# First attention of a two-block kernel: its weights turned by VectorE in 32x32 blocks with transfers through DRAM, its value products two units later, and the first block's tokens scaled once

## The reference, cut to what matters

```python
h = rms_norm(x, ln1_g)
z_a, z_b, z_c, z_g = split(h @ w_in)
# branch a: gelu, layer norm, chunked spatial gating, @ w_a_out
# branch b: p * sigmoid(g), causal depthwise convolution of 31 taps, layer norm, silu, @ w_b_out
# branch c, stick breaking attention, 8 heads of 64, for query block i:
z = einsum(q_blk, k[:ctx]) * scale
log_a = log_sigmoid(z) + (cs[..., -1:] - cs)      # cs: running sum of masked log_sigmoid(-z)
a = where(mask, exp(log_a), 0)
out = einsum(a, v[:ctx])                          # then @ w_c_out
merged = sum of sigmoid(z_g + b_gate) * y of the branches
x = x + merged @ w_out                            # then a feed-forward part
```

## Time and profile before

| | |
|---|---|
| median of 3 runs | 1275.33 us (1275.14 to 1275.87) |
| the profiled execution | 1275.76 us, its span 1274.0 us |
| TensorE busy | 1263.9 us, 99% of the span |
| VectorE, ScalarE, GpSimd busy | 869.3, 586.3 and 88.1 us |
| mean granted clock of TensorE | 0.999 |
| 16 DMA engines | 153.36 MB, 40.7% of their time by SP's queue |

### The profile page before, as it was taken

One profiled execution on the slowest core, in us unless ns is written; L12 is line 12 of the kernel. 1 busy time (PEld: TensorE's weight loads), 2 busy tenths in 40 slices (PEclk: granted clock), 3 DMA queues, 4 the chain that ended last, 5 costly groups with the idle time before them and its releaser, 6 DMA issues.

```text
span 1274.0 us, 15378 instructions
## 1 busy us (share of the span) xinstructions
PE 1263.9 (99%) x5760; PEld 1016.6 (80%) x5760; DVE 869.3 (68%) x1164; ACT 586.3 (46%) x866; POOL 88.1 (7%) x68
## 2 busy tenths in 40 slices
PE   8999999999999999999999999999999999999998
PEld 7888777888888888888888888888877777777886
DVE  5489899899877776666666333675469998655544
ACT  7235466232263443333333223512368899444223
POOL 0000222000000200000000001300012220000000
PEclk9999999999999999999999999999999999999999
DMA  7556222422322333323322222249825555665421
GB/s 264 178 130 172 66 67 67 165 97 77 120 75 97 99 100 99 99 99 99 98 91 102 90 88 91 99 125 215 239 76 124 140 159 131 183 148 149 161 70 67
DMA packets 220922, 153.36 MB, mean 120 GB/s; under 512 B 119704, under 2 KB 196416, under 8 KB 220608
## 3 DMA queue, kind: packets, MB, share of 16 engines
q1 hardware_dynamic: 220272, 151.53, 40.7%
q10 hardware_dynamic: 592, 1.05, 0.2%
HBM read 134.21 MB, written 18.35 MB: 120 GB/s over the span
## 4 chain that ended last, share of the span: by engine, by line
PE 97%; DVE 1%; DMA 1%; ACT 0%; SPq 0%; issue 0%; ACTq 0%
PE PS L1903 97%; PE PS L1970 1%; DMA STAGE<-in_w_in 1%; DVE WL L1163 0%; DVE XL L1201 0%; DVE XG L1193 0%; ACT XH L744 0%; ACT WH L716 0%; DVE TB L1752 0%; DVE XT L1896 0%; ACT SQF L1133 0%; DVE XT L1891 0%; DVE BLR L1790 0%; SPq L521 0%; SPq L520 0%
## 5 line engine op out<-in xcount | busy, mean ns | idle before, releaser
L716 ACT ACTIVATE WH<-STAGE 128x1024 fp32r<-128x1024 f32 x214 | 225.9, 1058 | 540.2 <-PE PS L1903 528.6
L1903 PE MATMUL PS<-XH,WH 128*128 128x512 f32 x960 | 380.9, 397 | 0.0
L1163 DVE TENSOR_TENSOR WL<-STAGE,WH 128x1024 fp32r<-128x1024 f32 x214 | 275.4, 1289 | 147.8 <-ACT WH L716 147.4
L1903 PE MATMUL PS<-XH,WL 128*128 128x512 f32 x960 | 373.9, 389 | 0.0
L1903 PE MATMUL PS<-XL,WH 128*128 128x512 f32 x960 | 373.8, 389 | 0.0
L1903 PEld LDWEIGHTS PS<-XH,WH 128*128 128x128 f32 x960 | 180.2, 188 | 43.5 <-issue 5.5
L1903 PEld LDWEIGHTS PS<-XL,WH 128*128 128x128 f32 x960 | 180.3, 188 | 39.0 <-issue 2.6
L1903 PEld LDWEIGHTS PS<-XH,WL 128*128 128x128 f32 x960 | 180.2, 188 | 38.1
L1903 PE MATMUL PS<-WH,XH 128*128 128x512 f32 x224 | 88.1, 393 | 0.6 <-DVE WL L1163 0.6
L1903 PE MATMUL PS<-WH,XL 128*128 128x512 f32 x224 | 87.2, 389 | 0.0
L1903 PE MATMUL PS<-WL,XH 128*128 128x512 f32 x224 | 87.2, 389 | 0.0
(11 more groups left out here) (289 smaller groups left out, 1782.3 us busy)
## 6 DMA issues: line engine op xcount, KB each, us to landing
STAGE<-in_w_in SPq DMA_DIRECT2D x51, 1024.0 KB, 5.2
STAGE<-in_w_up SPq DMA_DIRECT2D x22, 1024.0 KB, 5.1
STAGE<-in_w_down SPq DMA_DIRECT2D x11, 1024.0 KB, 5.0
probabilities<-TB SPq DMA_DIRECT2D x48, 128.0 KB, 5.8
PT<-probabilities SPq DMA_DIRECT2D x18, 256.0 KB, 5.6
STAGE<-in_w_out SPq DMA_DIRECT2D x4, 1024.0 KB, 5.3
STAGE<-in_w_rnn_out SPq DMA_DIRECT2D x4, 1024.0 KB, 5.3
STAGE<-in_w_attn_out SPq DMA_DIRECT2D x4, 1024.0 KB, 5.3
```

Source lines behind the costliest of these rows:

```text
L716: act.activation(ring(WH, n), staged(n), ACT.Copy).then_inc(hi_done, 1)
L1163: dve.tensor_tensor(ring(WL, n), staged(n), ring(WH, n).bitcast(F32), ALU.subtract)\
L1903: return pe.matmul(out_, lhsT, rhs, start=start, stop=stop, skip_group_check=True)
```

## The change

- Each token is scaled once. At the end of stage A VectorE multiplies `XG` with `RBC` in place (`x_scaled`, 8 instructions of 128x512), and ScalarE and VectorE split it anew into `XH`/`XL`, two channel tiles after each of the four last units that read the old ones (`x_scaled_high`, `x_scaled_low`). Unit 16 waits tile by tile for both parts. All units of stages B and C then come out scaled: the 8 drains to `TG0`/`TG1` and the 24 of the gates fall away, ScalarE reads PSUM itself, four drains become copies.
- The attention's weights are turned by VectorE in 32x32 blocks (`pair_turn` on VectorE, in the same step s+3, between mask and conversion) into `BTT`, two buffers and a third for the last step; SP stores them block by block to `AROW` in DRAM (`at_store`, 4 transfers of 128-byte pieces) and loads each head pair's three steps as rows to `AT` (`at_load`, 8 transfers). Both stand in SP's program behind the weight transfers 13 to 19 (`step` 0 to 6): stores after steps 3, 5, 7, 9, 11, 13 and 15 of VectorE, loads with those after steps 5, 9, 11 and 15.
- TensorE has no transposes there. The value products move from steps 6, 9, 12, 15 to 8, 11, 14 and 17, the last after the two quarter units 32 and 33.
- Taps: 2 in each step of stage B from i = 4 on (before 3, then 4), and 5, 5, 5, 5, 5, 3 in a half of stage C (before 4, 4, 4, 4, 6, 3).

```diff
+            def at_store(s):
+                sp.wait_ge(at_t, s + 1)
+                for a in range(4):
+                    sp.dma_start(AROW[s][0:2 * STEP_W[s % 3]].rearrange("(b i) (a j) -> a i b j", i=32, j=32)[a],
+                                 pair_tile(s)[32 * a:32 * a + 32].rearrange("p (b j) -> p b j", j=32))\
+                      .then_inc(at_out[s % 2], 16)
+            def at_load(p):
+                sp.wait_ge(at_out[0], 64 * ((3 * p + 2) // 2 + 1))
+                sp.wait_ge(at_out[1], 64 * ((3 * p + 1) // 2 + 1))
+                if p:
+                    sp.wait_ge(av_done, p)
...
@@ sync, in the loop over the weight transfers, behind transfer p
+                step = p - U_B // 2 - 5
+                if 0 <= step < 7:
+                    for s in ((0,), (1, 2), (3, 4), (5, 6), (7, 8), (9, 10), (11,))[step]:
+                        at_store(s)
+                    if step in (1, 3, 4, 6):
+                        at_load((1, 3, 4, 6).index(step))
@@ scalar
+            def x_scaled_high(u):
+                act.wait_ge(unit_done, U_B - 4 + u + 1)
+                for k in (2 * u, 2 * u + 1):
+                    act.wait_ge(xg_done, 2 * TT + k + 1)
+                    act.activation(XH[:, k, :], XG[:, k, :], ACT.Copy).then_inc(xh_tok, 1)
             for n in range(U_A, U_B):
+                if n == U_B - 1:
+                    x_scaled_high(3)
                 hi(n + 4)
+                if U_B - 4 <= n < U_B - 1:
+                    x_scaled_high(n - U_B + 4)
...
             def stick_act(i):
                 if 1 <= i < 13:
                     pair_sigmoids(i - 1)
-                if i >= 6 and i % 3 == 0:
-                    pair_out(i // 3 - 2)
-                if 3 <= i < 15:
-                    pair_turned(i - 3)
+                if i >= 8 and i % 3 == 2:
+                    pair_out((i - 8) // 3)
             for i in range(12):
                 hi(U_B + i + 4)
+                if i in (2, 3, 6, 7, 8, 9, 10, 11):
+                    act.wait_ge(unit_done, U_B + i + 1)
+                    if i >= 6:
+                        act.wait_ge(tg_used, (6, 7, 8, 9, 10, 11).index(i) + 1)
+                    act.activation((TG0, TG1)[i % 2][:], PS[:, i % 2, :],
+                                   ACT.Sigmoid if i < 8 else ACT.Gelu_apprx_tanh).then_inc(tg_act, 1)
@@ vector
+            def x_scaled(ks):
+                for k in ks:
+                    dve.tensor_tensor(XG[:, k, :], XG[:, k, :], RBC[:], ALU.mult).then_inc(xg_done, 1)
+            def x_scaled_low(u):
+                for k in (2 * u, 2 * u + 1):
+                    dve.wait_ge(xh_tok, 2 * TT + k + 1)
+                    dve.tensor_tensor(XL[:, k, :], XG[:, k, :], XH[:, k, :].bitcast(F32), ALU.subtract)\
+                       .then_inc(xl_tok, 1)
             for n in range(U_A, U_B + 4):
-                if n < U_B:
+                if n < U_B - 1:
                     lo(n + 4)
...
+                if n in (7, 9, 11):
+                    x_scaled({7: (0, 1, 2), 9: (3, 4), 11: (5, 6, 7)}[n])
+                if U_B - 4 <= n < U_B:
+                    x_scaled_low(n - U_B + 4)
+                if n == U_B - 1:
+                    lo(n + 4)
...
+            def pair_turn(s):
+                w = STEP_W[s % 3]
+                dve.wait_ge(a_ready, s + 1)
+                if 2 <= s < 11:
+                    dve.wait_ge(at_out[s % 2], 64 * (s // 2))
+                dve.transpose(pair_tile(s).rearrange("p (a c) -> p a c", c=w), BT[s % 2][:, :, 0:w])\
+                   .then_inc(at_t, 1)
...
                 if 2 <= i < 13:
                     pair_mask(i - 1)
+                if i >= 3:
+                    pair_turn(i - 3)
                 lo(U_B + i + 4)
@@ tensor
             def pair_values(p):
-                pe.wait_ge(at_ready, 4 * p + 4)
+                pe.wait_ge(at_ready, 128 * p + 128)
...
-                if i >= 6 and i % 3 == 0:
-                    pair_values(i // 3 - 2)
-                if 3 <= i < 15:
-                    pair_turn(i - 3)
+                if i >= 8 and i % 3 == 2:
+                    pair_values((i - 8) // 3)
+            def x_scaled_parts(k):
+                pe.wait_ge(xh_tok, 2 * TT + k + 1)
+                pe.wait_ge(xl_tok, 2 * TT + k + 1)
...
-                cm_unit(U_B + i, i % 2, XH, XL)
+                cm_unit(U_B + i, i % 2, XH, XL, 0, x_scaled_parts if i == 0 else None)
...
                     for u in range(2):
                         quad_unit(n0 + 6 * q + 4 + u, u, 4, BH, BL, KW)
+                    if b == 0 and q == 0:
+                        stick_pe(17)
```

More of the change, by code:

```diff
@@ L267, in program @@
                  for i in range(2)]
+        AROW = [nc.dram_tensor(f"attention_rows{i}", [1024, P], F32, kind="Internal").ap()
+                for i in range(12)]
         XROW = nc.dram_tensor("x_token_major", [SEQ, D], F32, kind="Internal").ap()
@@ L369, in keys_first, with pair_tile @@
             return PT[w % 2][:, kb, :]
+        def pair_tile(s):
+            return BTT[2 if s == 11 else s % 2][:, 0:2 * STEP_W[s % 3]]
         def parts_in(w):
@@ L493, in p_load @@
                       .then_inc(pt_in, 16)
+            def at_store(s):
[9 more added lines that the diff above has]
+                    sp.wait_ge(av_done, p)
+                for s in range(3 * p, 3 * p + 3):
+                    w = STEP_W[s % 3]
+                    for par in range(2):
+                        rows_ = AROW[s][par * w:(par + 1) * w].rearrange("(k p) c -> p k c", p=P)
+                        if s % 3 == 0:
+                            sp.dma_start(AT[:, par, 0:256].rearrange("p (k c) -> p k c", c=P), rows_[:, 0:2])\
+                              .then_inc(at_ready, 16)
+                            sp.dma_start(AT[:, par, 512:640], rows_[:, 2]).then_inc(at_ready, 16)
+                        elif s % 3 == 1:
+                            sp.dma_start(AT[:, par, 0:1152].rearrange("p (k c) -> p k c", c=384)[:, :, 256:384],
+                                         rows_).then_inc(at_ready, 16)
+                        else:
+                            sp.dma_start(AT[:, par, 384:1920].rearrange("p (k c) -> p k c", c=384)[:, :, 0:P],
+                                         rows_).then_inc(at_ready, 16)
             def q2_load(h):
@@ L865, in _ @@
                         hi(n + 4)
-                        if b == 0 and q == 0 and r < 4:
+                        if r < 4:
+                            act.wait_ge(unit_done, n + 1)
+                            if b or q:
+                                act.wait_ge(drained, DR_C + 8 * b + 4 * q - 4 + r + 1)
+                            bank = r % 2 if b == 0 and q == 0 else r
+                            act.activation(GS[:, r, :], PS[:, bank, :], ACT.Sigmoid,
+                                           bias=col(V_BG + BRANCHES[b] * KD + 4 * q + r))\
+                               .then_inc(gs_ready, 1)
+                        if b == 0 and q == 0:
                             stick_act(12 + r)
@@ L1428, in _ @@
                 if i >= 4:
-                    taps(3 if i < 6 else 4)
+                    taps(2)
                 if 1 <= i < 13:
@@ L1444, in _ @@
                         dve.wait_ge(unit_done, n + 1)
-                        if r < 4:
-                            if b or q:
-                                dve.wait_ge(drained, DR_C + 16 * b + 8 * q - 4 + r + 1)
-                            bank = r % 2 if b == 0 and q == 0 else r
-                            dve.tensor_tensor(GS[:, r, :], PS[:, bank, :], RBC[:], ALU.mult)\
-                               .then_inc(drained, 1)
                         if b == 0 and q == 0 and r == 0:
                             pair_mask(11)
+                        if b == 0 and q == 0 and r < 3:
+                            pair_turn(9 + r)
                         lo(n + 4)
@@ L1456, in _ @@
                         if r == 5:
+                            if b == 0 and q == 0:
+                                dve.wait_ge(at_out[0], 64 * 6)
+                                dve.wait_ge(at_out[1], 64 * 6)
                             for m in range(4):
@@ L1471, in _ @@
                                .then_inc(bl_ready, 1)
-                        taps((4, 4, 4, 4, 6, 3)[r])
+                        taps((5, 5, 5, 5, 5, 3)[r])
             assert taps_done == KW * CVK
@@ L2057, in pair_scores @@
                 last.then_inc(sc_done, 1)
-            def pair_turn(s):
-                pe.wait_ge(a_ready, s + 1)
-                if s:
-                    pe.wait_ge(at_ready, s + (s + 2) // 3)
-                else:
-                    pe.wait_ge(sg_read, 4)
-                for par in range(2):
-                    for z in range(STEP_W[s % 3] // P):
-                        last = tr(PS[:, 4 + par, z * P:(z + 1) * P], BT[s % 2][:, par, z * P:(z + 1) * P])
-                last.then_inc(at_t, 1)
             def pair_values(p):
-                pe.wait_ge(at_ready, 4 * p + 4)
```

(5 more changed lines are left out.)

107 lines of the change are left out of this document (45 added, 62 removed).

## The result

The changed kernel takes 1298.39 us (median of 4 runs, 1296.79 to 1301.06) against 1275.27 (1275.14 to 1275.87): ratio 1.0182, 95% interval 1.0165 to 1.0200. The forecast was 1290 us, in a range of 1279 to 1297: the sign is right, the loss of 23.1 us is 8.3 larger than the sum of 14.8, and the time lies 1.4 above the range. The profiled execution of the changed kernel took 1298.17, its span is 1296.1 (before 1274.0): the rows have to explain 22.1 us.

A forecast was written before the change was run, and what follows sets the result against it. TensorE, busy 1263.9 of 1274.0 us, was taken to bound the kernel. Removed transposes (-8.4) and added waits and clock loss summed to +14.8 us, so 1290 us, range 1279 to 1297.

The forecast's parts named there:

- scores of step 6: TensorE's scores wait for sigmoids behind turn 3, which waits until store 1 has landed: +1.2 us.
- scores of step 8: TensorE's scores come at 176.5, not 175.1, because turn 5 waits for store 3: +1.5 us.
- scores of step 10: TensorE's scores come at 193.4, not 189.8, because turn 7 waits for store 5: +3.6 us.
- second value product: TensorE wants it at 194.3, but load 1 waits for store 5 and lands at 197.1: +2.9 us.
- last value product: TensorE stands at 236.2 until load 3 lands at 245.7: +9.5 us (bounds 5 and 12).
- clock: TensorE's slower clock after the longest wait: +1.5 us (bounds 0 and 5, if shorter waits lose it too).
- Removed, and stage A: 80 transposes gone from TensorE, -8.4 us; stage B's first unit waiting for split tokens, +2.1; gating products late, +0.9.
- rival 4: Removed transposes worth their 280 ns record each, giving back 22.4 us: 1276.1 us; chance 0.05 with all else within 0.2%.
- The trip: Through DRAM: store lands 8.1 us after its weights' issue (three-block 7.4), the load takes 6.3 more (bounds 5.2 and 9).
- Half clock after each wait: Part of the rival for worse: TensorE at half clock after each wait, trips under load, over 1297 us; chance 0.06.
- The deciding place: Whether all transfers hide is decided there: 4.9 us from weights 19's issue to use, weights alone take 5.2.
- The rival that all transfers are hidden: All stores and loads of the turned weights hidden: -8.4 + 3.0 = -5.4 us, 1269.9 us; chance 0.10.

The follow-up runs named there:

- scaling alone: Changed kernel with TensorE turning the first attention's weights and ScalarE copying them as before, nothing stored or loaded; 1278.80 us.
- no trip: Changed kernel without the twelve stores and four loads of the turned weights, AT set to zero, VectorE still turning all steps; 1271.82 us.
- both_first: Changed kernel with stores and loads of the turned weights issued ahead of the conversion's wait and the 1 MB of weights; 1272.45 us.
- values_later: Changed kernel with the last value product one unit (5.44 us) later; 1293.72 us.
- four buffers: Changed kernel with four turn buffers in place of two, the queue's order unchanged; 1297.88 us.
- both_first_values_later: Kernel of both_first with the last value product one unit later; 1270.36 us.
- fill_waits: Changed kernel with products of no use put into TensorE's stream at four of its waits; 1297.05 us.
- last_first_filled: Changed kernel with only the last store and load ahead of the weights, plus useless products at TensorE's first three filled waits; 1289.31 us.
- early_first_filled: Kernel of early_first with 44 products of no use ahead of TensorE's wait for the last load; 1283.37 us.
- early_first: Changed kernel with all stores and loads of the turned weights except the last ahead of the weights; 1284.47 us.

## Why the prediction was wrong in size and right in sign

The chain of waits of the changed kernel carries the dates (start, us, what; L568 issues weights, L507 stores, L1453 is VectorE's turn):

```profile
148.26 0.39 SPq L568
...
152.16 5.29 DMA attention_rows<-BTT
...
183.61 0.39 SPq L568
...
185.21 3.75 SPq L507
...
191.62 2.13 DMA attention_rows<-BTT
...
197.08 4.26 DMA AT<-attention_rows
...
229.99 1.16 DVE BTT L1453
...
236.73 0.39 SPq L568
...
242.02 3.11 DMA attention_rows<-BTT
...
248.64 3.92 DMA AT<-attention_rows
```

| term of the sum | forecast | rows of the changed kernel |
|---|---|---|
| 80 transposes | -8.4 | -7.8 (scaling alone against no trip) |
| unit 16 | +2.1 | +1.6 |
| gating products | +0.9 | +0.7 |
| scores of step 6 | +1.2 | +2.8 |
| scores of step 8 | +1.5 | 0 |
| scores of step 10 | +3.6 | +5.2 |
| second value product | +2.9 | +2.2 |
| quarter products | not seen | +1.75 |
| last value product | +9.5 | +8.5 |
| clock | +1.5 | 3.0 + 0.7 + 1.6 + 1.6 = +6.9 |
| sum | +14.8 | +21.9 of 22.1 in the spans |

The table lists every place; the same chain, read by its dates, tells which terms carried the time to the last value product:

| date (us) | forecast | changed kernel | later by, new in this line |
|---|---|---|---|
| weights issued after conversion 29 | 182.8 | 183.6 | 0.8 |
| load 1 landed (second value product) | 197.1 | 201.3 | 3.4 |
| weights issued after conversion 35 | 231.3 | 236.7 | 1.2 |
| load 3 landed (last value product) | 245.7 | 252.6 | 1.5 |

The last value product starts 6.9 us later than forecast, and the span's loss is 7.3 larger than the sum. 4.9 of the 6.9 are the two trips on this path: 17.7 us and 15.9 us from the weights' issue to the load's landing, where I had 14.4 for each. **That is the step that failed: the cost of a trip was put too low**, for the store (about 2.1 us of the 4.9) and for the load (about 2.7), which takes 7.7 us in both_first too, with nothing ahead of it. With the forecast's trips the time would by this estimate have been about 1293.5, inside the range. The clock term, 5.4 us too low in the table, is the larger miss in the list but gave back little time where it was removed (see **Clock** below).

- **Removed, and stage A**: right, within 0.6 each. Had the transposes been worth their record of 280 ns (rival 4), the two kernels with and without them would be 22 us apart, and they are 7.0.
- **The trip**, the term mis-sized. I took 7.4 us from the weights' issue to the landing of a three-block store and 8.1 for a four-block one. By the chain it was 9.2 (148.26 to 157.5, store 1, three blocks), 9.9 (183.61 to 193.5, store 5, four) and 8.4 (236.73 to 245.1, store 11, four), and 7.6 for store 3 (three), whose rows are left out. Except for step 11 two steps' stores are issued together, and SP stands up to 3.75 us in the issue of one transfer (185.21); my pattern was one store alone. The load took 7.9 and 7.4 in place of 6.3, which I had scaled from one transfer in one piece.
- **Scores of step 10**: besides the trip I left out what ScalarE does between a turn and its sigmoids. Its timeline:

```profile
194.63 1.28 ACT L863 ACT_TABLE_LOAD   x1 [5.77 <-DVE BTT L1453]
195.92 0.81 ACT L863 ACTIVATE GB<-PS 128x768 f32<-128x768 f32 x1
```

  After each GELU it loads the sigmoid's table again, 1.28 us, and here that came behind the wait, on the path. In the kernel before it took the same 1.28 us and TensorE did not wait for it. Beside the 1.28 us the rows show next to nothing for the switch: the sigmoid starts 1.29 us after the load's start, and the next load, at 198.39, starts 0.01 us after the copy before it ends.
- **Scores of step 8**: the half clock after step 6 had made TensorE so late that nothing was left to wait for. Without it (values_later) the wait is 2.75 us. I had moved TensorE's dates by the waits that I knew, and not by the clock.
- **Quarter products**: a wait that the diff shows and I had not walked through. ScalarE's copy of the third value product writes where the second turn buffer lies and waits for store 9 (ScalarE stands idle for 7.34 us before 232.30, until that store has landed); I put the third values at 0 because their load is early, and did not ask what their copy waits for.
- **Clock**: no run shows the 1.5 us that the sum has for one wait; it was my estimate. The first transposes, 0.23 us against 0.13 each, don't carry it: the kernel before has a granted clock of 1.00 from 1 to 7 us, where both lie. In the changed kernel there were three stretches of half clock, and the first alone had 6 us of work at half speed: 9.53 - 6.52 = 3.0; at the others 0.73 for the scores (1.65 - 0.92) and 1.6 twice for the value products (3.97 - 2.38, and the same from 201.38 on). "Half clock after each wait" stood as a rival of 0.06; by the rows it happened at the waits of 2.8, 5.2 and 8.5 us, if not in every execution (0.93 us for the eight scores after 2.88 in values_later). But it isn't what put the total outside: of the 6.9 us the 3.0 after step 6 stood in place of a wait, and with full clock at the first three waits the time was still 1297.05.
- **The sum as such**: it closes within 0.2 us, in part by luck: the changed execution began stage B 0.6 us sooner than the one before (unit 16 at 99.83, then 100.46), so the rows owe 22.7. And its terms are not prices. Taking away the terms for scores (four buffers, 8 us) or the early half clock (fill, 5.3 us) moved the time by 0.5 and 1.3. Each term is what TensorE waited for last at that place; under most of them lies another, with nearly the same date, because all hang on one queue. In the prediction's own working two terms are 0.1 larger than the dates beside them give (1.4 for the scores of step 8, 2.8 for the second value product), which changes nothing.
- **The deciding place**: I had named the last value product. Its trip moved alone was worth 8.9 of the 23.1 us; the trips before it, moved without it, 13.9. So it was the largest single wait, and not the one place that decides.

The rival that all transfers are hidden (1269.9) is what both_first_values_later reaches (1270.4), by the route that the prediction named for it, the stores past the weights.

## What to carry to other kernels

A transfer that another engine waits for doesn't belong behind a bulk prefetch, nor behind the prefetch's own wait, in the same queue's program: the same stores and loads ahead of both (the two are not separated here) turned a loss of 1.8% into a gain of 0.2%, and of 0.4% with the last product one unit later. Before adding buffers against a wait, look what would be waited for in its place; if it hangs on the same queue, as here, the buffers can buy nothing (1297.88 us with four, 1298.39 with two). To forecast such a chain, carry the dates from one trip to the next and price a trip by rows with the same pieces and the same traffic ahead of it. A wait of TensorE like these can bring a stretch of half clock behind it (6 us of work at 0.50 behind 2.81 us); where the next thing that it needs is late anyway, that time does not come back if only the clock is mended (1.3 us of the 6.9 in fill_waits).

## What the runs showed of the hardware that was not expected

- The clock can outlast its cause: in the changed kernel TensorE waited 2.81 us, the clock fell about as the wait ended, and it ran at half for 6 us of full work. But the same wait of 2.88 us in values_later was followed by full clock (0.93 us for the eight scores, not 1.65). The value products took 4.06 us after a wait of 1.90 in last_first_filled, 3.56 after 2.56 in fill_waits, and 2.38 after 2.37 in early_first_filled. The length of the wait alone doesn't tell these apart; what does is open.
- SP's issue of a DMA is not always 0.5 us: the third of a store's four transfers held it for 3.75 us (185.21 in the chain above), with the weights and two transfers of 1024 packets each ahead of it. The four issues of store 11 took 5.42 us in the changed kernel, behind the weights, and 2.24 in both_first, where these had arrived. Such a store delays whatever SP has to issue next, here the fourth transfer, to 189.00.
- The profiled spans of equal kernels differ by up to 1 us before any of this begins: in early_first unit 16 started at 101.13 us, in early_first_filled at 100.06; ScalarE's second piece of weights, for which it waits on a DMA, starts at 9.73 and 8.67. Differences of that size were judged by the runs, not by the spans.
